# Two down-projection loads per expert are issued by ScalarE instead of SyncE

## The reference, cut to what matters

```
hgu = xb @ w_up_gate[e] + b_up_gate[e]          # 1024 x 2048 weights, 8 MB
x_glu = jnp.minimum(hgu[:, :D_EXPERT], SWIGLU_LIMIT)
x_lin = jnp.clip(hgu[:, D_EXPERT:], -SWIGLU_LIMIT, SWIGLU_LIMIT)
hact = x_glu * jax.nn.sigmoid(SWIGLU_ALPHA * x_glu) * (x_lin + 1.0)
return hact @ w_down[e] + b_down[e]             # 1024 x 1024 weights, 4 MB
```

## Time and profile before

| | us |
|---|---|
| median of three runs | 1588.45 (1587.61 to 1588.86) |
| the profiled execution | 1587.67 |
| its span, from the first to the last instruction | 1585.9 |
| around the span | 1.77 |
| mean granted TensorE clock, share of full | 0.991 |
| TensorE matmuls busy | 1460.3 |
| VectorE, ScalarE, GpSimd busy | 480.8, 413.2, 458.5 |

### The profile page before, as it was taken

How to read it: one execution, slowest core, us unless ns; L and a number is a source line. 1 busy time by engine, 2 the same in 40 slices (tenths; PEclk the granted TensorE clock), 3 DMA queues, 4 the chain that set the end, 5 groups by cost and what they waited for, 6 DMA issues and landing times.

```text
span 1585.9 us, 18697 instructions
## 1 busy us (share of the span) xinstructions
PE 1460.3 (92%) x7536; PEld 827.3 (52%) x7537; DVE 480.8 (30%) x847; ACT 413.2 (26%) x534; POOL 458.5 (29%) x355
## 2 busy tenths in 40 slices
PE   8999999988988888989888988889899999999998
PEld 6877533333333333333323333333698776799986
DVE  5536412121121121121121121122567586323211
ACT  6354301001001010010010010011754834453332
POOL 7836000000000000000000000001687763779994
PEclk9999999999999999999999999999999999999999
DMA  9533899999999999999999999999565332545540
GB/s 345 200 117 98 361 429 428 428 427 428 426 427 427 429 428 427 426 428 428 428 426 427 426 429 428 428 427 400 171 211 162 106 107 79 194 153 186 186 160 27
DMA packets 91415, 502.31 MB, mean 317 GB/s; under 512 B 7947, under 2 KB 38275, under 8 KB 66499
## 3 DMA queue, kind: packets, MB, share of 16 engines
q1 hardware_dynamic: 89840, 498.71, 77.9%
q10 hardware_dynamic: 1491, 2.36, 0.5%
HBM read 500.00 MB, written 1.05 MB: 316 GB/s over the span
## 4 chain that ended last, share of the span: by engine, by line
PE 53%; DMA 37%; DVE 3%; ACT 3%; issue 2%; SPq 1%; POOL 0%; ACTq 0%; DVEq 0%
DMA ring<-in_w_up_gate 35%; PE PS L931 14%; PE PS L546 9%; PE PS L548 9%; PE PS L547 9%; PE PS L951 4%; PE PS L958 1%; PE PS L898 1%; DMA ring<-in_w_ple_gate 1%; SPq L429 1%; PE PS L1197 1%; ACT w_high L1321 1%; DMA ring<-in_w_in 1%; ACT arena L1333 0%; PE PS L940 0%
## 5 line engine op out<-in xcount | busy, mean ns | idle before, releaser
L2424 POOL TENSOR_TENSOR w_low<-ring,w_high 128x512 fp32r<-128x512 f32 x343 | 447.2, 1341 | 1098.9 <-ACT w_high L1321 1098.5
L931 PE MATMUL PS<-ring,arena 128*64 128x512 f32 x2048 | 463.7, 603 | 54.1 <-DMA ring<-in_w_up_gate 54.1
L931 PEld LDWEIGHTS PS<-ring,arena 128*64 128x64 f32 x2048 | 141.4, 138 | 360.5 <-issue 259.3
L951 PE MATMUL PS<-ring,arena 128*64 128x512 f32 x1024 | 227.0, 595 | 28.1 <-ACT arena L1507 27.9
L1498 ACT ACTIVATE arena<-arena 128x512 f32<-128x512 f32 x32 | 20.1, 629 | 756.8 <-DVE arena L2048 756.8
L1321 ACT ACTIVATE w_high<-ring 128x2048 fp32r<-128x2048 f32 (+1 forms) x87 | 162.6, 1880 | 124.0 <-PE PS L548 100.8
L2048 DVE TENSOR_SCALAR arena<-PS 128x512 f32<-128x512 f32 x32 | 22.1, 692 | 466.4 <-PE PS L931 466.4
L951 PEld LDWEIGHTS PS<-ring,arena 128*64 128x64 f32 x1024 | 72.9, 137 | 160.1 <-issue 158.7
L546 PE MATMUL PS<-w_high,XNT_h 128*128 128x512 f32 (+1 forms) x336 | 136.4, 406 | 6.1 <-DVE XNT_l L1757 5.1
L546 PE MATMUL PS<-XNT_h,w_high 128*128 128x256 f32 (+1 forms) x464 | 130.7, 282 | 2.2 <-DVE XNT_l L1740 1.3
L548 PE MATMUL PS<-w_high,XNT_l 128*128 128x512 f32 (+1 forms) x336 | 132.0, 393 | 0.0
(11 more groups left out here) (381 smaller groups left out, 1440.8 us busy)
## 6 DMA issues: line engine op xcount, KB each, us to landing
ring<-in_w_up_gate SPq DMA_DIRECT2D x127, 2048.0 KB, 25.4
ring<-in_w_down SPq DMA_DIRECT2D x64, 2048.0 KB, 23.1
ring<-in_w_in SPq DMA_DIRECT2D x33, 1024.0 KB, 5.5
ring<-in_w_gate_up SPq DMA_DIRECT2D x22, 1024.0 KB, 5.2
ring<-in_w_down SPq DMA_DIRECT2D x11, 1024.0 KB, 4.9
ring<-in_w_out SPq DMA_DIRECT2D x8, 1024.0 KB, 4.9
ring<-in_w_ple_gate SPq DMA_DIRECT2D x4, 1024.0 KB, 22.8
ring<-in_w_ssd_proj SPq DMA_DIRECT2D x4, 1024.0 KB, 5.3
```

Source lines behind the costliest of these rows:

```text
L931: ins = nc.tensor.matmul(PS[64 * (n % 2):64 * (n % 2) + 64, 4 + n // 2, :], x, w[:, n * 512:(n + 1) * 512], start=False, stop=c == KC - 1, ...
L951: ins = nc.tensor.matmul(PS[64 * n:64 * n + 64, 7, :], lhs, w[:, k, n * 512:(n + 1) * 512], start=(j, k) == (0, 0), stop=(j, k) == (1, 3))
L2424: ins = nc.gpsimd.tensor_tensor(LOW[raw_slot(key)][:, at], slot(raw_slot(key))[:, at], HIGH[m % BUF][:, at].bitcast(F32), ALU.subtract)
```

## The change

SyncE issues only the four up pairs of experts 1 to 31 (`UPS` is 4). The two down pairs of experts 1 to 31 are issued by ScalarE, in its own loop over the experts, behind the copy L1507 of the expert before and behind a wait on `w_used` for the same counts as before. The places, the semaphores and the sizes of the loads stay as they are. The last expert's ScalarE work stands behind the loop. The first expert's loads and the second pass are unchanged.

```diff
-            def expert_loads(e, turn):
-                for j in range(PER_EXPERT):
+            def expert_loads(e, turn, pairs=PER_EXPERT):
+                for j in range(pairs):
 
                     sp.wait_ge(sem("w_used"), turn * PER_EXPERT + (before_experts - PER_EXPERT + j + 1))
                     expert_load(e, j)
...
             with sp.Fori(1, E - 1) as e:
-                expert_loads(e, e)
-            expert_loads(E - 1, E - 1)
+                expert_loads(e, e, UPS)
+            expert_loads(E - 1, E - 1, UPS)
...
-            with act.Fori(0, E) as e:
+
+            def expert_act(e):
+
                 sigmoid("glu", "sig", e + 1)
                 act.wait_ge(sem("spread"), e + 1)
                 nc.scalar.activation(SPT, PS[:, 7, 0:256], ACT.Copy).then_inc(sem("sT_slots"), 1)
                 act.wait_ge(sem("hT_ps"), e + 1)
                 nc.scalar.activation(HTS, PS[:, 6, :], ACT.Copy).then_inc(sem("hT"), 1)
+
+            with act.Fori(0, E - 1) as e:
+                expert_act(e)
+                for j in range(2):
+                    s = EXPERT_SLOT[UPS + j]
+                    act.wait_ge(sem("w_used"), e * PER_EXPERT + (before_experts + UPS + j + 1))
+                    src = w_down_e[e + 1, j * 512:(j + 1) * 512, :].rearrange("(p k) n -> p (k n)", p=P)
+                    act.dma_start(slots2(s), src).then_inc(landed[s], 16)
+            expert_act(E - 1)
```

## The result

| | before | after |
|---|---|---|
| median, us | 1588.29 (1587.61 to 1588.86, 4 runs) | 1597.61 (1595.62 to 1598.51, 4 runs) |
| ratio to before | | 1.0065, interval 1.0051 to 1.008 |
| the profiled execution, its span | 1587.67, 1585.9 | 1596.92, 1595.1 |
| mean granted TensorE clock | 0.991 | 0.977 |

The changed kernel is slower by 9.3 us in the medians (0.59%) and by 0.65% in the ratio. The two spans differ by 1595.1 - 1585.9 = 9.2 us.

What follows compares the result with a forecast made beforehand. The prediction took the full DMA engines (share 1.01, 427 GB/s) to bound the expert stage; 0 + 0 + 9.6 - 0.5 = +9.1 us on 1587.67 gave 1596.8, stated as 1597, range for 8 in 10 1588 to 1612.

Steps and rivals of the forecast that it cites:

- SyncE's and ScalarE's issues: Expert loop: moving 62 issues from SyncE to ScalarE, with 62 waits, neither gains nor costs time, 0 us.
- Equal shares: DMA engines in the expert stage: both queues, when loaded, are served side by side in equal shares; no size of its own.
- no change: Rival, DMA queues: downs land no earlier against the ups than now, by age, favoured ups or late issues; 1588, chance 0.13.
- U3 lands last: Each expert's loads: U3 lands behind both downs, 9.8 us later than before.
- U1, U2, U3 remain: Each expert, when its downs are issued: U0 is nearly in and three up pairs are still to come, 14.7 us of stream.
- The stream doesn't dry up: Middle of the expert stage: 8.5 us of backlog keeps the engines busy, an expert still takes 29.4 us, no loss.
- a bound on the end: End of the experts: U3 may be late only in every second expert; if expert 30 has the late one, +8.2 us.
- The end of the experts: Expert 31: 13.2 us of TensorE work follow the last landing, U3's second half, against 3.6 before, +9.6 us.
- The gate stage: Second run of matmuls behind the experts: the hold by the last `ple_gate` piece is gone, -0.5 us.
- Nothing later: After the gate stage's second run of matmuls: nothing takes up the rest of the delay, which passes on to the end.
- Faster: Rival, expert-stage stream: two queues carry more than one, deciding from 433 GB/s on; 1584 at that rate, chance 0.06.
- Much slower: Rival, middle experts: idle engines or TensorE as the bound cost 0.5 us per expert, 15.5 us in all; 1612, chance 0.17.

Runs made afterwards that it cites:

- the first run: Changed kernel, but the down pairs of experts 28 to 31 are issued by SyncE again: 1587.56 us, ratio 1.0009 to the kernel before.
- the second: Kernel before, but only expert 31's two down pairs are issued by ScalarE: 1599.85 us, ratio 1.0076.
- the third: Changed kernel, but in experts 1 to 31 SyncE issues U0, U2, D0 and ScalarE U1, U3, D1: 1593.93 us, ratio 1.0033.
- the fourth run: Changed kernel, but ScalarE issues a next expert's downs only when its U2 has landed: 1594.06 us, ratio 1.0056.

## Why the prediction was right

**SyncE's and ScalarE's issues: 0.** No run tests the issue cost by itself. But the first run has 54 of ScalarE's 62 issues and the time of the kernel before, so they cost nothing that can be measured. ScalarE's row in the changed kernel shows where they lie:

```profile
602.72 3.86 ACTq L1517 DMA_DIRECT2D ring<-in_w_down  x2
606.99 1.28 ACT L1498 ACT_TABLE_LOAD   x1 [8.33 <-PE PS L951]
```

The sigmoid's table load now stands behind the two waits, and it is done at 608.3, 16 us ahead of the U3 matmuls (624.30).

**Equal shares: right in the middle, not at the end.** In the middle, while both queues hold loads of 2 MB, two stretches of 3 us of the changed kernel (609 to 612, 615 to 618; packets, MB, share of the engines) read:

```profile
q10 hardware_dynamic: 44, 0.72, 56.4%
q1 hardware_dynamic: 39, 0.57, 44.9%
```

```profile
q1 hardware_dynamic: 48, 0.70, 55.1%
q10 hardware_dynamic: 51, 0.57, 45.1%
```

In six such stretches from 606 to 624 neither queue gets more than 58%. The Trainium skill (DMA: Bandwidth & Descriptors, section "Queues, rings and completion order") says that each engine takes turns between its queues, a packet at a time; the trace agrees, with 44 to 58%. That is what lets a down pair that is issued behind an up pair finish ahead of it. The rival "no change" rested on an order by age, which these rows exclude. But in the last expert, from 1088 to 1092 us, the shares are far from equal:

```profile
q10 hardware_dynamic: 81, 1.20, 70.4%
q1 hardware_dynamic: 80, 0.51, 30.6%
```

The two queues still move as many packets, 81 and 80. But U3 comes there as two loads of 1 MB, whose packets carry less, 0.51 MB in 80 against 1.20 MB in 81. So it is the packets that are shared equally here, and the bytes only where the packets of both queues are alike.

**U3 lands last: right in the last expert alone.** The prediction had U3 land behind both downs in every expert. In experts 1 to 30 D1 is the last, 2.4 to 11.6 us behind U3. Of expert 30, U3 (issued at 1041.39) and D1 (issued at 1052.65), with the us to landing at the end:

```profile
ring<-in_w_up_gate SPq DMA_DIRECT2D x1, 2048.0 KB, 24.0
ring<-in_w_down ACTq DMA_DIRECT2D x1, 2048.0 KB, 20.1
```

So U3 landed at 1065.4 and D1 at 1072.7. The step that failed is "U1, U2, U3 remain": D0's first packets came some 3 us after its issue, with U1 in, so that two pairs, not three, were left against the two downs. In the last expert U3's second half does come last, at 1099.2, behind D1 at 1097.4; its smaller packets are the likely reason, which no run tests. The order on which the +9.6 rests thus came out as foretold where it counts, but by luck as much as by the reasoning.

**The stream doesn't dry up: right.** Share 1.01 at 427 GB/s from 200 to 1075 us, and the first run's 1.0009. The alternation of late and early U3 was foretold in a bound on the end; in the middle it means one wait, of up to 6.1 us, in about every second expert.

**The end of the experts: +9.6 foretold, +8.0 measured.** The work left behind the last landing is as foretold, and the size was off by 1.6. Of this, 1.3 is the time of the last landing, taken as 1100.6 and measured as 1099.27; the distance behind it was 12.9 instead of 13.2. Why the stream ended 1.3 us earlier is not settled; the first run, whose last experts load as in the kernel before, has its last landing 0.9 us earlier too (1099.71), so executions may differ by this much. The bound for the clock in this stretch was not needed: the 16 matmuls of U3 took 5.64 us, with a pause for the second half in it.

**The gate stage: -0.5 foretold, -0.6 measured.** As foretold, VectorE's piece (L1768, L1757 before) no longer waits for ScalarE: it starts right behind its own chain, at 1121.65, 7.4 us later than it did, and the matmuls follow 1.26 us later, where it was 1.27. The wait is put down to GpSimd's splitting there, which ended at the same time, so a faster VectorE would no longer help alone.

**Nothing later: wrong by 1.6.** The prediction let the rest pass unchanged to the end, but the L573 stretch lost 1.6 us more to the clock. This and the 1.6 too many at the end of the experts cancel, which is why the sum, 9.1, came so near the 9.2 measured. The forecast's size is thus partly luck. Its sign is not, and the first two runs show its place.

**The other rivals.** Faster would have needed 433 GB/s: the two queues moved 427 together. Much slower would have needed idle engines in the middle, or TensorE as the bound there: the share stayed at 1.01, and the first run, with the long waits of 27 experts, lost nothing that can be measured.

## What to carry to other kernels

Where one queue already filled the DMA engines (a share of 1.01), a second one added no bandwidth here; it only changed the order of arrival, as both queues took turns by packets. Look for the transfer whose landing leaves the most work to do, and make sure that nothing overtakes it at the end of the stream; in the middle, the backlog hid the reordering. To see it, compare the distance from the last landing to the end of the stage (3.6 and 12.9 us), not the sum of the waits, which was nearly the same here. A shorter distance is worth only as much as the engine really waits for that landing: D1 in halves saved 0.4 us, not 1.8. And put fillers only where a trace shows the wait: those ahead of U3 added their own time to the loss that they were to measure.

## What the runs showed of the hardware

The clock fell in one of two nearly equal situations. In the 10 us ahead of the L573 transposes, TensorE was busy for 6.88 us in both kernels and idle for the last 2.2; the clock granted behind them was 1.00 before and 0.66 after. Before (10 us ahead, then 5 us behind):

```profile
1132.60:1142.60 10.00, 6.88 (x32) 4.80 (x30) 6.20 (x18) 9.07 (x17) 5.57 (x6) 1.00 0.87 280
1142.90:1147.90 5.00, 4.93 (x26) 4.16 (x27) 2.17 (x9) 3.98 (x9) 0.93 (x4) 1.00 0.18 52
```

After:

```profile
1140.00:1150.00 10.00, 6.88 (x32) 4.80 (x30) 6.21 (x18) 9.06 (x17) 5.59 (x6) 1.00 0.87 278
1150.00:1155.00 5.00, 4.65 (x18) 4.07 (x19) 2.46 (x9) 3.49 (x9) 1.03 (x3) 0.66 0.19 52
```

The other traces have the same transposes, with 2.2 us idle ahead of them in all. Of the eleven traces, the clock granted in the 5 us behind was 0.66 to 0.68 in four (the changed kernel, the second, the third and the fourth run) and 1.00 in seven. So the 1.6 us does not come in every execution, and neither the busy nor the idle time ahead of it could have foretold it.
